# State space model's coefficients on four quarters of the array, and the last expert weights in fewer parts

## The chip, the cores and the metric

The kernel runs on one core of a Trainium2 chip. Its time is the device time of one execution in microseconds (us). Before the change it is 2480.15 us, the median of 3 runs (2478.76 to 2482.7). Engines are named as in the profile: PE is TensorE (PEld its weight loads), DVE VectorE, ACT ScalarE, POOL GpSimd, SP SyncE, which here issues most DMAs. Everything is computed in fp32; one fp32 matmul of the program is two MATMUL instructions in the trace, each with a weight load of its own.

## The reference

Two transformer-like blocks over 512 tokens of 1024 channels. The first has sparse attention beside a recurrent branch and an MLP. The second has a Fourier mix beside a state space model (SSM), and 64 experts, two per token. What matters here is one direction of the SSM, and the experts:

```
def _ssm_direction(ug, a_re, a_im, log_dt, b_re, b_im, c_re, c_im, reverse):
    lam = lax.complex(a_re, a_im);  dt = exp(log_dt)[:, None]
    a_bar = jnp.exp(lam * dt)                                  # 32 groups, 64 states
    b_bar = ((a_bar - 1.0) / lam)[..., None] * b_mat           # 16 channels per group
    bu = jnp.einsum('blgc,gnc->blgn', ug, b_bar)
    _, h = lax.associative_scan(_scan_combine, (a, bu), axis=1, reverse=reverse)
    return jnp.einsum('blgn,gcn->blgc', h, c_mat).real

def expert_block(args):
    xb, e = args
    a = jax.nn.silu(xb @ w_gate[e]) * (xb @ w_up[e])
    return a @ w_down[e]
```

It runs once forwards and once backwards, and the two are added. Everything that depends only on the weights (powers of a_bar, b_bar, C, and products of them) is a coefficient, independent of the tokens.

## The kernel before, in words

The program is written engine by engine; the order on each engine is the order of the code, and semaphores tie them together. PSUM has 8 banks of 512 columns; open_tile (L372) takes a bank and waits until its last user was evicted. Weights come in 2 MB loads into slots of SBUF, issued by SP in a fixed plan (L344 to L356); a load waits until the product that last used its slot has ended.

**Coefficients.** They are computed during the first block's MLP, woven (L135) into its first product, mlp_in, whose 32 dense tiles (8 matmuls of 128x512 each, L381) PE does one after the other. Both scans share the 128 partitions: the 64 states of the forward scan stand in rows 0 to 63, those of the backward scan in rows 64 to 127. BB holds b_bar (real and imaginary, 32 groups x 16 channels), CC holds C. The sequence is cut into blocks of 8 tokens, so for each group a 16 x 272 table z is needed: 128 columns from the one scan, 16 from both (the token itself), 128 from the other. In 8 steps c of four groups each:

- DVE and POOL form outer products of powers with BB and CC: Mr and Mi (to be transposed) and mb = MB2[c % 2], C times the powers; S("mcm") tells that mb is there (L1830 to L1842, L2258).
- PE transposes Mr and Mi, two banks (L660, L663), and after the next dense tile multiplies for z: for each group six matmuls into one bank of its own, in output rows 0 to 15 (L667 to L680). The operand on the array is BZ, a copy of BB with zeros in the other scan's rows, so that a product over all 128 rows takes one scan alone. Two groups come after one dense tile and two after the next.
- ACT evicts the transposes and each group's z (L1280) into Zt, and stores mbr, mbi, mcr, mci and z to DRAM, five stores per step, counted on st0 and st1 (16 each, so 80 per step; 320 in all on each).

BZ is zeroed by POOL (L2270) and filled by DVE with four copies (L1804, L1805). Zt is one buffer. SP, POOL and ACT wait for 320 on both counts before they go on to the second block.

**Experts.** 32 pairs of experts; a pair has six 2 MB matrices (gate, up, down for both), 192 loads through a ring of 9 slots (L2444 to L2458). pe_pair (L983) transposes the pair's rows, multiplies by gate and up (L1005), transposes, and multiplies by down (L1034). The two experts of a pair have 64 rows each and sit on the two halves of the array's columns. For the last pair the two up matrices are loaded in 8 parts of 512 KB, k by k and expert by expert (S("up0") to S("up3")), and the two down matrices in the same way ("last0" to "last3"); before either set SP waits for both slots (L2459 to L2470). PE takes them part by part (L1003, L1018; the down product at L1022). After it come DVE's and ACT's evictions (L2204, L1430), the spreading of the last pair's rows to the tokens by one-hot products (L981), DVE's sums with the rows that POOL gathers from y_d (L2128, L2320), and the final norm (L2212).

Of the kernel before, what the change touches and what calls it, by code (L numbers as in the profile page):

```python
# [16 lines left out]
PAIRS = 32  # L17
# [131 lines left out]
def program(nc, A, out):  # L149
    with ExitStack() as ctx:  # L150
# [36 lines left out]
        zone = al(53000 - at[0])  # L187
# [79 lines left out]
        BZ = view(zone, 20480, 4, 512)  # L267
        T1, T2, Mr, Mi = (view(zone, 20480 + 2048 + 512 * n, 512) for n in range(4))
        Zt = view(zone, 20480 + 4096, 1088)
# [108 lines left out]
        def tensor_program(pe):  # L378
# [272 lines left out]
            def ssm():  # L651
                yield from pause(8)
                flat = BB.rearrange("p a b c -> p a (b c)")
                for c in range(8):
# [12 lines left out]
                    for q in range(4):  # L667
                        gg = 4 * c + q
                        o = open_tile(pe, ("z", gg), any_bank())
                        cols = slice(16 * gg, 16 * gg + 16)  # L670
                        mm_ = (mb[:, 0, 128 * q:128 * q + 128], mb[:, 1, 128 * q:128 * q + 128])
                        for at0, n, zr, zi, rhs in (
                                (0, 128, BZ[:, 2, cols], BZ[:, 3, cols], mm_),
                                (128, 16, flat[:, 0, cols], flat[:, 1, cols], (CC[:, 0, gg, :], nC[:, cols])),
                                (144, 128, BZ[:, 0, cols], BZ[:, 1, cols], mm_)):
                            pe.matmul(o[0:16, at0:at0 + n], zr, rhs[0], start=True, stop=False)  # L676
                            ins = pe.matmul(o[0:16, at0:at0 + n], zi, rhs[1], start=False, stop=True)
                        ins.then_inc(T.f("z", gg), 1)
                        if q == 1:
                            yield  # L680
                    yield
# [301 lines left out]
        def pe_pair(pe, table, q, ready, weight, bank, gathered):  # L983
# [9 lines left out]
            for mat, name in enumerate(("g", "u")):  # L993
# [5 lines left out]
                for k in range(8):  # L999
                    if mat == 0 and k % 4 == 0:  # L1000
                        pe.wait_ge(*table.free("xt", q, k // 4))
                    if parts and k % 2 == 0:
                        pe.wait_ge(S(f"up{k // 2}"), 32)  # L1003
# [46 lines left out]
        def scalar_program(act):  # L1050
# [193 lines left out]
            def ssm():  # L1244
# [11 lines left out]
                for c in range(8):  # L1256
# [5 lines left out]
                    if c > 1:  # L1262
                        act.wait_ge(st, 80 * (c // 2))
# [1466 lines left out]
```

## Time and profile before

| | |
|---|---|
| three runs, median (lowest, highest) | 2480.15 us (2478.76, 2482.7) |
| the profiled execution | 2475.58 us, span 2473.8 us |
| mean granted TensorE clock | 0.967 |
| PE busy | 2260.6 us, 91% of the span |
| DVE, ACT, POOL busy | 613.6, 331.4, 208.9 us |
| moved by DMA | 552.44 MB |
| chain that ended last | PE 70%, DMA 24% |

The span runs from the first to the last instruction of the program. A busy share is an average over stages with different limits, so it says little about one stage. A row of the chain is a piece of work that the end of the kernel waited for; a row of the timeline gives start, duration, engine, line and operation, and in brackets how long the engine had been idle and what released it. In the windows PEclk is the granted clock as a share of 2.4 GHz, and the DMA share the mean over 16 engines.

### The profile page before, as it was taken

Reading aid. Unit: us, or ns where it says so; the run is one execution under the profiler, and the core shown is the slowest. Engines: PE = TensorE matmul, PEld = TensorE weight load, DVE = VectorE, ACT = ScalarE, POOL = GpSimd, SP = SyncE. Lnnn points to the kernel's source line nnn. Section 1 sums busy time; section 2 is a strip of 40 time slices with the busy share of each in tenths; the row PEclk is TensorE's granted clock in tenths of the full one; section 3 lists DMA queues with packets and bytes.
Section 4 is the critical chain, followed back from the end, with each engine's and each line's share of the span. In section 5 each row is a group of like instructions: output and inputs, shape, how many; then the busy total and the mean of one; then the engine's idle time right before and its main releaser. Section 6 shows DMA issues by size and latency. Waiting matters only on the chain.

```text
span 2473.8 us, 20406 instructions
## 1 busy us (share of the span) xinstructions
PE 2260.6 (91%) x8284; PEld 1048.6 (42%) x8284; DVE 613.6 (25%) x1315; ACT 331.4 (13%) x668; POOL 208.9 (8%) x187
## 2 busy tenths in 40 slices
PE   8999999999999999999999999988788888878786
PEld 5554444445455544457644454333333333333332
DVE  2146544301623130032631142111111111111114
ACT  2014424202111100021010030000000000000001
POOL 0001111010333200000000000000000000000001
PEclk9999999999999999998999999999999988898998
DMA  6201010322232221128432429999999999999995
GB/s 270 85 35 68 35 68 8 146 102 85 85 106 88 112 105 68 68 73 134 151 123 85 170 108 407 425 426 427 426 426 426 427 426 426 424 426 423 423 397 219
DMA packets 70288, 552.44 MB, mean 223 GB/s; under 512 B 21416, under 2 KB 25640, under 8 KB 38768
## 3 DMA queue, kind: packets, MB, share of 16 engines
q1 hardware_dynamic: 43680, 515.49, 51.3%
q10 hardware_dynamic: 16432, 23.23, 3.1%
q0 software_dynamic: 10080, 12.38, 1.4%
q8 instruction: 67, 1.10, 0.2%
q14 instruction: 29, 0.24, 0.0%
HBM read 543.91 MB, written 35.68 MB: 234 GB/s over the span
## 4 chain that ended last, share of the span: by engine, by line
PE 70%; DMA 24%; DVE 2%; SPq 1%; ACT 1%; issue 1%; DVEq 0%; POOL 0%; ACTq 0%; POOLq 0%
PE ps L381 25%; DMA sb<-in_eu 11%; PE ps L457 9%; PE ps L1005 8%; PE ps L697 8%; DMA sb<-in_eg 6%; DMA sb<-in_ed 6%; PE ps L1034 4%; PE ps L400 2%; PE ps L855 2%; PE ps L629 2%; PE ps L542 1%; PE ps L575 1%; PE ps L569 1%; PE ps L676 1%
## 5 line engine op out<-in xcount | busy, mean ns | idle before, releaser
L381 PE MATMUL ps<-sb 128*128 128x512 f32 (+2 forms) x1536 | 613.8, 559 | 2.9 <-issue 1.4
L1005 PE MATMUL ps<-sb 128*64 128x512 f32 x2048 | 478.6, 623 | 89.4 <-DMA sb<-in_eu 63.3
L381 PEld LDWEIGHTS ps<-sb 128*128 128x128 f32 x1536 | 279.7, 190 | 317.4 <-issue 314.2
L1005 PEld LDWEIGHTS ps<-sb 128*64 128x64 f32 x2048 | 175.0, 143 | 372.3 <-issue 372.2
L1034 PE MATMUL ps<-sb 128*64 128x512 f32 x992 | 249.5, 661 | 38.0 <-DMA sb<-in_ed 26.2
L457 PE MATMUL ps<-sb 128*128 128x512 f32 x512 | 238.2, 604 | 0.0
L697 PE MATMUL ps<-sb 128*128 128x512 f32 x448 | 192.5, 592 | 0.7 <-issue 0.7
L1034 PEld LDWEIGHTS ps<-sb 128*64 128x64 f32 x992 | 81.0, 151 | 185.0 <-issue 166.8
L1448 DVE TENSOR_TENSOR sb<-sb 128x32 f32<-128x32 f32 (+10 forms) x292 | 115.4, 412 | 136.6 <-PE ps L663 83.2
L457 PEld LDWEIGHTS ps<-sb 128*128 128x128 f32 x512 | 92.1, 191 | 101.0 <-issue 99.7
L697 PEld LDWEIGHTS ps<-sb 128*128 128x128 f32 x448 | 85.0, 190 | 107.7 <-issue 107.7
L2324 POOL DMA_INDIRECT y_d<-sb x31 | 31.2, 1007 | 854.0 <-PE ps L991 742.4
L1064 ACT ACTIVATE sb<-ps 128x512 f32<-128x512 f32 (+4 forms) x119 | 62.5, 532 | 268.1 <-PE ps L381 91.2
L2196 DVE SCALAR_TENSOR_TENSOR sb<-sb,ps 128x512 f32<-128x512 f32 x32 | 22.1, 690 | 273.4 <-PE ps L1005 273.4
L2191 DVE SCALAR_TENSOR_TENSOR sb<-sb,ps 128x512 f32<-128x512 f32 x32 | 22.1, 690 | 241.0 <-ACT sb L1420 241.0
L1472 DVE COPY sb<-ps 128x512 f32<-128x512 f32 (+6 forms) x53 | 34.5, 650 | 163.0 <-PE ps L381 89.8
L2241 POOL TENSOR_TENSOR sb<-sb 128x256 f32<-128x256 f32 (+3 forms) x32 | 41.6, 1301 | 381.8 <-DVE sb L1666 381.7
L2206 DVE COPY sb<-ps 128x512 f32<-128x512 f32 x31 | 21.5, 693 | 209.1 <-PE ps L1034 209.1
L2186 DVE TENSOR_TENSOR sb<-ps,sb 128x512 f32<-128x512 f32 x64 | 41.4, 687 | 101.9 <-PE ps L991 101.1
L1424 ACT ACTIVATE sb<-ps 128x512 f32<-128x512 f32 x32 | 19.2, 599 | 347.5 <-PE ps L1012 347.5
L400 PE MATMUL ps<-sb 128*128 128x256 f32 x256 | 58.6, 389 | 6.3 <-DVE sb L1467 3.5
L855 PE MATMUL ps<-sb 128*128 128x512 f32 x128 | 58.4, 598 | 1.6 <-DVE sb L1987 1.6
(286 smaller groups left out, 1554.3 us busy)
## 6 DMA issues: line engine op xcount, KB each, us to landing
sb<-in_eg SPq DMA_DIRECT2D x64, 2048.0 KB, 33.0
sb<-in_eu SPq DMA_DIRECT2D x62, 2048.0 KB, 33.7
sb<-in_ed SPq DMA_DIRECT2D x62, 2048.0 KB, 33.9
sb<-in_m SPq DMA_DIRECT2D x16, 2048.0 KB, 7.3
sb<-in_mg SPq DMA_DIRECT2D x8, 1536.0 KB, 6.9
sb<-in_winF SPq DMA_DIRECT2D x5, 2048.0 KB, 7.3
sb<-in_mgg SPq DMA_DIRECT2D x4, 2048.0 KB, 7.3
sb<-in_wo SPq DMA_DIRECT2D x4, 2048.0 KB, 7.3
```

The source lines that it names most:

```text
L381: ins = pe.matmul(out, lhsT, rhs, start=k == 0, stop=k == len(pieces) - 1)
L400: ins = pe.matmul(T.ap(*tile)[:, t], lhsT, rhs[:, t], start=k == 0, stop=k == 7)
L457: ins = pe.matmul(o, lhsT, rhs, start=k == 0, stop=k == 7)
L629: ins = pe.matmul(o, MG1[:, k, 128 * i:128 * i + 128], wo[nh][:, k, :], start=k == 0, stop=k == 7)
L697: ins = pe.matmul(acc[2 * i + nh], HT[:, k, 128 * i:128 * i + 128], w[:, q, 512 * nh:512 * nh + 512], start=k == 0, stop=False)
L855: ins = pe.matmul(T.ap(*name), MG2[:, k, 128 * i:128 * i + 128], wo[nh][:, k, :], start=k == 0, stop=k == 7)
L1005: ins = pe.matmul(o[64 * e:64 * e + 64, :], x[:, k, 64 * e:64 * e + 64], weight(2 * mat + e)[:, 512 * k:512 * k + 512], start=k == 0, stop ...
L1034: ins = pe.matmul(o[64 * e:64 * e + 64, :], aT[:, k, 64 * e:64 * e + 64], weight(4 + e)[:, d:d + 512], start=k == 0, stop=k == 3)
L1064: act.activation(dst, T.ap(*name) if src is None else src, ACT.Copy).then_inc(T.s(*name), 1)
L1448: return own(dve.tensor_tensor(o, a, b, op))
L2186: dve.tensor_tensor(XT[:, 4 * hf:4 * hf + 4, :], table.ap("xt", q, hf).rearrange("p (a b) -> p a b", a=4), bc(ck("gx")[:, 4 * hf:4 * hf + ...
L2241: pool.tensor_tensor(pr, pr, bc(ST[u % 4][:, 2:4], 2, nk), ALU.mult).then_inc(S("prob"), 1)
```

## The change

In the coefficients, the four groups of a step go to the four quarters of the array's columns, output rows 32q to 32q + 15, and each scan is multiplied with its own 64 rows alone, taken straight from BB; BZ, its memset and its copies go. Each step fills two banks, ("zb", c, 0) with the backward scan (128 columns) and the part of both scans (16 columns), and ("zb", c, 1) with the forward scan. ACT evicts each bank with one copy over all 128 partitions into Zt, which is now doubled, and issues four stores for z, one per group; the counts become 128 per step and 512 in all.

For the last pair, the first expert's up matrix comes in one load of 2 MB and the second's in two of 1 MB; the first's down matrix in one of 2 MB and the second's in parts of 1 MB, 512 KB and 512 KB. Each expert's load waits for its own slot only. PE's waits are changed to match.

```diff
-        BZ = view(zone, 20480, 4, 512)
-        Zt = view(zone, 20480 + 4096, 1088)
+        Zt = [view(zone, 20480 + 4096 + 272 * n, 272) for n in range(2)]
...
@@ PE, ssm()
                     pe.wait_ge(S("mcm"), c + 1)
-                    for q in range(4):
-                        gg = 4 * c + q
-                        o = open_tile(pe, ("z", gg), any_bank())
-                        cols = slice(16 * gg, 16 * gg + 16)
-                        mm_ = (mb[:, 0, 128 * q:128 * q + 128], mb[:, 1, 128 * q:128 * q + 128])
-                        for at0, n, zr, zi, rhs in (
-                                (0, 128, BZ[:, 2, cols], BZ[:, 3, cols], mm_),
-                                (128, 16, flat[:, 0, cols], flat[:, 1, cols], (CC[:, 0, gg, :], nC[:, cols])),
-                                (144, 128, BZ[:, 0, cols], BZ[:, 1, cols], mm_)):
-                            pe.matmul(o[0:16, at0:at0 + n], zr, rhs[0], start=True, stop=False)
-                            ins = pe.matmul(o[0:16, at0:at0 + n], zi, rhs[1], start=False, stop=True)
-                        ins.then_inc(T.f("z", gg), 1)
-                        if q == 1:
-                            yield
-                    yield
+                    cols = [slice(16 * (4 * c + q), 16 * (4 * c + q) + 16) for q in range(4)]
+                    for way, rows_ in enumerate((slice(64, 128), slice(0, 64))):
+                        o = open_tile(pe, ("zb", c, way), any_bank())
+                        for ri in range(2):
+                            for q in range(4):
+                                ins = pe.matmul(o[32 * q:32 * q + 16, 0:128], flat[rows_, ri, cols[q]],
+                                                mb[rows_, ri, 128 * q:128 * q + 128], start=ri == 0, stop=ri == 1)
+                        if way == 0:
+                            for ri in range(2):
+                                for q in range(4):
+                                    rhs = nC[:, cols[q]] if ri else CC[:, 0, 4 * c + q, :]
+                                    ins = pe.matmul(o[32 * q:32 * q + 16, 128:144], flat[:, ri, cols[q]], rhs,
+                                                    start=ri == 0, stop=ri == 1)
+                        ins.then_inc(T.f("zb", c, way), 1)
+                        yield
...
@@ PE, pe_pair, the last pair's up
-                    if parts and k % 2 == 0:
-                        pe.wait_ge(S(f"up{k // 2}"), 32)
+                    if parts and k == 0:
+                        pe.wait_ge(S("up0"), 16)
+                    if parts and k % 4 == 0:
+                        pe.wait_ge(S(f"up{1 + k // 4}"), 16)
...
@@ and its down, for k in range(4)
-                    pe.wait_ge(S(f"last{k}"), 32)
+                    if k != 1:
+                        pe.wait_ge(S(f"last{max(k, 1)}"), 16)
+                    if k == 0:
+                        pe.wait_ge(S("last0"), 16)
...
@@ ACT, ssm()
-                    if c:
-                        act.wait_ge(S(f"st{(c - 1) % 2}"), 80 * ((c - 1) // 2 + 1))
-                    for q in range(4):
-                        gg = 4 * c + q
-                        copy(("z", gg), Zt[0:16, 272 * q:272 * q + 272], T.ap("z", gg)[0:16, 0:272])
-                        if q == 1:
-                            yield
-                    for q in range(4):
-                        act.wait_ge(*T.free("z", 4 * c + q))
-                    act.dma_start(z_d[:, gs, :], Zt[0:16, :].rearrange("p (a b) -> p a b", a=4)).then_inc(st, 16)
+                    copy(("zb", c, 0), Zt[c % 2][:, 0:144], T.ap("zb", c, 0)[:, 0:144])
+                    yield
+                    copy(("zb", c, 1), Zt[c % 2][:, 144:272], T.ap("zb", c, 1)[:, 0:128])
+                    for way in range(2):
+                        act.wait_ge(*T.free("zb", c, way))
+                    for q in range(4):
+                        act.dma_start(z_d[:, 4 * c + q, :], Zt[c % 2][32 * q:32 * q + 16, :]).then_inc(st, 16)
...
@@ DVE (its four copies into BZ and the wait for the memset go as well, and POOL's memset)
-                    dve.wait_ge(*T.full("z", 4 * (c - 2) + 3))
-                    dve.wait_ge(S(f"st{c % 2}"), 80 * (c // 2))
+                    dve.wait_ge(*T.full("zb", c - 2, 1))
+                    dve.wait_ge(S(f"st{c % 2}"), 128 * (c // 2))
...
@@ SP, the last pair
-            for e in range(2):
-                sp.wait_ge(*T.full(*W.ended[W.before[("ex", 6 * PAIRS - 4 + e)]]))
-            for k in range(4):
-                for e in range(2):
-                    sp.dma_start(slot("ex", 6 * PAIRS - 4 + e)[:, 1024 * k:1024 * k + 1024],
-                                 EW[1][2 * PAIRS - 2 + e][:, 1024 * k:1024 * k + 1024]).then_inc(S(f"up{k}"), 16)
...
+            for mat, sem, parts in ((1, "up", (2048, 2048)), (2, "last", (2048, 1024, 1024))):
+                n = 6 * PAIRS - 6 + 2 * mat
+                sp.wait_ge(*T.full(*W.ended[W.before[("ex", n)]]))
+                sp.dma_start(slot("ex", n), EW[mat][2 * PAIRS - 2]).then_inc(S(f"{sem}0"), 16)
+                sp.wait_ge(*T.full(*W.ended[W.before[("ex", n + 1)]]))
+                at_ = 0
+                for k, size in enumerate(parts):
+                    sp.dma_start(slot("ex", n + 1)[:, at_:at_ + size], EW[mat][2 * PAIRS - 1][:, at_:at_ + size]).then_inc(S(f"{sem}{k + 1}"), 16)
+                    at_ += size
```

## Rows read from the trace of the kernel before

**Rows 1.** The page: PE's busy row, and what the DMA engines moved in 40 slices.

```profile
PE 2260.6 (91%) x8284; PEld 1048.6 (42%) x8284; DVE 613.6 (25%) x1315; ACT 331.4 (13%) x668; POOL 208.9 (8%) x187
...
GB/s 270 85 35 68 35 68 8 146 102 85 85 106 88 112 105 68 68 73 134 151 123 85 170 108 407 425 426 427 426 426 426 427 426 426 424 426 423 423 397 219
```

**Rows 2.** The page: the chain that ended last, shares by engine.

```profile
PE 70%; DMA 24%; DVE 2%; SPq 1%; ACT 1%; issue 1%; DVEq 0%; POOL 0%; ACTq 0%; POOLq 0%
```

**Rows 3.** Chain in order of time, 690 to 720 us: start, us, piece.

```profile
690.73 0.44 PE ps L660 x4
...
691.60 6.87 PE ps L381 x16
698.47 0.32 PE ps L676 x2
698.79 0.22 PE ps L677 x2
...
699.05 0.05 PE ps L677 x2
...
700.52 7.06 PE ps L381 x16
...
716.70 0.44 PE ps L660 x4
```

**Rows 4.** Line L676: duration in ns, minimum, median, maximum, and shapes.

```profile
L676 PEld LDWEIGHTS ps<-sb x192: 92/96/97, 672.4 to 864.9; 128*16 128x16 f32 x192
L676 PE MATMUL ps<-sb x192: 176/270/283, 672.4 to 865.0; 128*16 128x128 f32 x128, 128*16 128x16 f32 x64
```

**Rows 5.** Timeline of PE: products on the two halves of the array.

```profile
2389.55 7.09 PE L1005 MATMUL ps<-sb 128*64 128x512 f32 x32 [0.94 <-DMA sb<-in_eg]
```

**Rows 6.** Waits from 640 to 895 us: total us, times, longest.

```profile
ACT sb L1241 <- PE ps L381: 174.5, 27, 6.7
...
DVE sb L1448 <- PE ps L663: 83.2, 6, 14.4
```

**Rows 7.** Waits of PE from 866 to 1490 us, the longest.

```profile
PE ps L400 <- DVE sb L1467: 3.5, 1, 3.5
...
PE ps L743 <- DMA sb<-mbi_d: 1.1, 1, 1.1
```

**Rows 8.** DMA issues by size: count, KB each, median us to landing.

```profile
sb<-in_ed SPq DMA_DIRECT2D x62, 2048.0 KB, 33.9
...
sb<-in_ed SPq DMA_DIRECT2D x8, 512.0 KB, 12.9
```

**Rows 9.** Timeline of the SP queue, 2384 to 2460 us.

```profile
2396.72 16.61 SPq L2463 DMA_DIRECT2D sb<-in_eu  x8
2413.43 13.53 SPq L2469 DMA_DIRECT2D sb<-in_ed  x8
```

**Rows 10.** Windows: us, PE, PEld, DVE, ACT, POOL busy; PEclk, DMA share, GB/s.

```profile
2405.00:2415.00 10.00, 8.37 (x42) 3.22 (x40) 1.01 (x2) 0.60 (x1) 0.00 (x0) 1.00 0.73 261
...
2425.00:2435.00 10.00, 9.06 (x45) 3.57 (x42) 1.38 (x2) 0.60 (x1) 5.01 (x5) 1.00 0.99 368
...
2445.00:2450.00 5.00, 2.75 (x8) 0.53 (x6) 0.00 (x0) 0.00 (x0) 0.00 (x0) 0.50 0.25 102
```

**Rows 11.** Timeline, 2434 to 2462 us: last down product (L1022) and VectorE.

```profile
2436.01 1.94 PE L1022 MATMUL ps<-sb 128*64 128x512 f32 x8 [0.69 <-ACT sb L1424]
...
2438.67 1.94 PE L1022 MATMUL ps<-sb 128*64 128x512 f32 x8 [0.72 <-DMA sb<-in_ed]
...
2443.55 1.28 DVE L2128 SCALAR_TENSOR_TENSOR sb<-sb 128x1024 f32<-128x1024 f32 x1 [1.26 <-DMA sb<-y_d,sb]
...
2443.77 2.73 PE L1022 MATMUL ps<-sb 128*64 128x512 f32 x8 [3.16 <-DMA sb<-in_ed]
...
2448.74 3.34 PE L1022 MATMUL ps<-sb 128*64 128x512 f32 x8 [2.25 <-DMA sb<-in_ed]
...
2450.77 0.75 DVE L2204 TENSOR_SCALAR sb<-ps,sb 128x512 f32<-128x512 f32 x1 [5.93 <-PE ps L1022]
```

More of the change, by code:

```diff
@@ L1262, in ssm @@
                     if c > 1:
-                        act.wait_ge(st, 80 * (c // 2))
+                        act.wait_ge(st, 128 * (c // 2))
                     if c == 0:
@@ L1292, in row_load @@
                 act.dma_start(row, A[name].partition_broadcast(P)).then_inc(S("row"), 16)
-            act.wait_ge(S("st0"), 320)
-            act.wait_ge(S("st1"), 320)
+            act.wait_ge(S("st0"), 512)
+            act.wait_ge(S("st1"), 512)
             act.wait_ge(S("ep"), 1)
@@ L1800, in vector_program @@
             after(tt(BB[:, 1], v32(Mr), v32(Mi), ALU.add))
-            flat = BB.rearrange("p a b c -> p a (b c)")
-            dve.wait_ge(S("bz_zero"), 1)
-            for ri in range(2):
-                own(dve.tensor_copy(BZ[0:64, ri, :], flat[0:64, ri, :]))
-                after(own(dve.tensor_copy(BZ[64:128, 2 + ri, :], flat[64:128, ri, :])))
             dve.tensor_scalar(nC, CC[:, 1].rearrange("p a b -> p (a b)"), -1.0, None, ALU.mult).then_inc(S("ssm_k"), 1)
@@ L2269, in ssm @@
                 pool.wait_ge(*T.full("wo1", 3, 1))
-                pool.memset(BZ, 0.0).then_inc(S("bz_zero"), 1)
                 yield
@@ L2282, in gpsimd_program @@
             weave(mlp_in(), ssm())
-            pool.wait_ge(S("st0"), 320)
-            pool.wait_ge(S("st1"), 320)
+            pool.wait_ge(S("st0"), 512)
+            pool.wait_ge(S("st1"), 512)
             pool.memset(Ep[:, 0, :, 0], 1.0).then_inc(S("ep_one"), 1)
@@ L2401, in sync_program @@
             sp.wait_ge(S("mg1"), 8)
-            sp.wait_ge(S("st0"), 320)
-            sp.wait_ge(S("st1"), 320)
+            sp.wait_ge(S("st0"), 512)
+            sp.wait_ge(S("st1"), 512)
             for g in range(2):
@@ L2458, in sync_program @@
                     load(("ex", n), EW[k // 2][2 * q + k % 2])
-            for e in range(2):
-                sp.wait_ge(*T.full(*W.ended[W.before[("ex", 6 * PAIRS - 4 + e)]]))
-            for k in range(4):
-                for e in range(2):
-                    sp.dma_start(slot("ex", 6 * PAIRS - 4 + e)[:, 1024 * k:1024 * k + 1024],
-                                 EW[1][2 * PAIRS - 2 + e][:, 1024 * k:1024 * k + 1024]).then_inc(S(f"up{k}"), 16)
-            for e in range(2):
-                sp.wait_ge(*T.full(*W.ended[W.before[("ex", 6 * PAIRS - 2 + e)]]))
-            for k in range(4):
-                for e in range(2):
-                    sp.dma_start(slot("ex", 6 * PAIRS - 2 + e)[:, 1024 * k:1024 * k + 1024],
-                                 EW[2][2 * PAIRS - 2 + e][:, 1024 * k:1024 * k + 1024]).then_inc(S(f"last{k}"), 16)
+            for mat, sem, parts in ((1, "up", (2048, 2048)), (2, "last", (2048, 1024, 1024))):
[7 more added lines that the diff above has]
+                    at_ += size
             sp.wait_ge(*T.full("g", PAIRS - 1))
```

## The prediction

> **What bounds the kernel now.** I read the page first: PE is busy for 91% of the span, and from slice 25 of 40 on the DMA engines move some 425 GB/s [rows 1]. The chain that ended last is PE for 70% and DMA for 24% [rows 2]. So two regimes follow each other: PE sets the time up to the experts, and the stream of expert weights sets it from there to the last pair. The stream's first loads wait for ring slots that earlier products release, so an earlier PE moves the stream forward as a whole.
>
> For the first edit I took the chain in order of time inside the MLP's first product, where the coefficients are woven in. The reader is to see that it is PE without a gap: dense tiles of 16 instructions (an fp32 matmul is two) in 6.87 to 7.06 us, and between them a half of a step's four groups, from 698.47 to 700.52 us [rows 3]. ACT and DVE wait for PE there, 174.5 and 83.2 us in all, DVE up to 14.4 us at a time [rows 6]. For the second edit I took the timeline of the last pair: the last down product waits three times for its parts [rows 11].
>
> **Edit 1, the products on quarters.** One of the 8 steps takes 716.70 - 690.73 = 25.97 us. Off go the transposes (0.87, from 690.73 to 691.60) and three dense tiles at 6.87: 4.49 us are left for the coefficients [rows 3]. A step holds 32 instructions with 128 columns (128 of L676 [rows 4] and as many of L677 over 32 groups are 8 per group) and 16 with 16 columns. The former cost 0.22 / 2 = 0.11 us, the latter 0.05 / 2 = 0.025 [rows 3]: 3.52 + 0.40 = 3.92. The other 0.57 I put down to the four changes between the full array and its 32-column tiles, 0.14 each.
>
> The changed step has just as many instructions, 32 and 16, so nothing is saved unless they overlap. Each matmul still streams 128 columns; half the rows make none of them shorter. What changes is that four of them in a row write four quarters of the array's columns, where now all sit in the first quarter. The nearest thing that the trace shows is the experts' product on halves: 32 instructions of 512 columns take 7.09 us [rows 5], where 16 full ones take 6.87 [rows 3]. Two halves thus run side by side at next to no loss. It shows no quarters, and none on 64 rows with 32 columns. Bounds: none overlap, 3.52 us; all four do, 0.88. In between, two at a time, 1.76. I take 0.88, since the halves come within 4% of their ideal, and since four instructions per 0.11 us is 0.027 each, not quicker than the 0.025 at which the small ones already follow each other. For the small ones I keep 0.40 (bound below 0.10 for full overlap; above, 0.40). The changes of tile become five (64 rows, 128 rows, full, 64 rows, full): 0.71. The sum is 0.88 + 0.40 + 0.71 = 1.99 us against 4.49, so 2.50 saved per step and **20.0 us** over eight. With the small ones overlapped too it would be 22.4; two at a time, (4.49 - 1.76 - 0.40 - 0.71) x 8 = 13.0; no overlap, 4.49 - 4.63 = -0.14 per step, a loss of 1.1 us.
>
> The weight loads stay one per instruction. One of them takes 95 ns and lies beside the instruction before it [rows 4]. The Trainium skill (TensorE: Matmul & The Clock Gate, Part 3, What overlaps and what doesn't) speaks against this change: it says that a weight load overlaps running matmuls only where the row group differs, and the four quarters share their rows. The trace disagrees for halves, which share all 128 rows and still pack [rows 5]; for quarters it shows nothing. The same page (Measured speedup vs the span model) gives 2.38 for three column tiles; an estimate with that efficiency is 3.52 / 3.17 = 1.11 us per step in place of 0.88, and 1.8 us less gain.
>
> What the rest of edit 1 touches lies off the path. ACT makes two copies per step in place of four and issues four stores in place of one, 24 issues more in all, in a stage in which it waits for PE for 174.5 us [rows 6]; behind them in its queue stand the Relu evictions of the dense tiles, which have all other banks of the ring to be late in. A step needs 4 banks in place of 6. The waits on the stores count to 512 in place of 320; what they gate (POOL's and DVE's table of powers, SP's next loads) has the MLP's whole second product before it is needed. DVE loses four copies and the wait for POOL's memset, where it already is ahead of PE [rows 6]. All at nothing; if DVE were late, its own slack of up to 14.4 us per step would have to go first, and the steps shrink by 2.5.
>
> Does the gain survive? From 866 to 1490 us PE's longest wait is 3.5 us, for DVE; the one for a DMA is 1.1 us, behind a load that a product itself releases [rows 7]. All of this moves with PE. I carry the 20.0 whole.
>
> **Edit 2, the last weights.** Now 16 transfers of 512 KB, issued in 16.61 and 13.53 us [rows 9]; 2.1 and 1.7 us each, while SP is held. Changed: one of 2 MB and two of 1 MB for up; one of 2 MB, one of 1 MB and two of 512 KB for down. Seven issues, and the first waits for its own slot only. In the windows in which small parts are moved, the engines' share falls to 0.73 with 261 GB/s, and at share 0.99 they move 368 GB/s, where the slices before show 424 or so [rows 1, 10]. A 2 MB load takes 33.9 us to land, at 4.9 us each (2.10 MB at 426 GB/s) [rows 1, 8]: seven are under way, so low shares mean that some engines have run dry while others are behind, and a load lands with the slowest. Feeding the fast ones better therefore doesn't help by itself; bigger pieces do. 8.4 MB at 368 GB/s are 22.8 us; half of it at 426, 3.1 MB halfway at 397 and 1.05 MB at 368 are 20.6: **2.2 us**. The last parts moreover land 5.1 and 5.0 us apart (2438.67, 2443.77, 2448.74 [rows 11]), twice what 1.05 MB needs, since the gathers of the rows of y share the engines; parts that land earlier leave less beside them.
>
> The end sees it through two waits. The last product's four parts start at 2436.01, 2438.67, 2443.77 and 2448.74 and run 1.94, 1.94, 2.73 and 3.34 us, the last with a granted clock of 0.50, the lower level of 1.2 GHz, from 2445 to 2450 [rows 10]. Without any wait the product would take 7.1 us (as 32 instructions on halves do, [rows 5]), end at 2443.1 and gain 9.0 us: the upper bound. But DVE takes the gathered rows first, until 2443.55 + 1.28 = 2444.83, and only then evicts the product, now at 2450.77 [rows 11]; with the gathers where they are, 5.9 is the most. The lower bound is 0: were the transfers no faster at all, part 1 would wait for six of the eight half megabytes and start about when the third does now, 2443.77; four parts at 1.77 us end at 2450.9, not after 2452.1. So the coarser first part costs nothing by itself. I take **4.5 us**, between 2.2 and 5.9, nearer to the latter since a late part also costs the lower clock (3.34 us in place of 1.77). SP's other queue entry, the final norm's row, follows seven issues and not sixteen; it is needed last.
>
> **Sum.** 20.0 + 4.5 = 24.5 us. The profiled execution took 2475.6 us, its span 2473.8: it would take 2451.1. The three timed runs have a median of 2480.15, 4.6 higher, which I leave in: 2480.15 - 24.5 = **2455.7 us**.
>
> **Rivals.** (a) Only two quarters run at a time, because each fp32 matmul is two instructions on one tile and matmuls start in order. For it: they are issued tile by tile. Against: on halves the order is the same and nothing is lost. 13.0 + 4.5: 2462.7. (b) Nothing overlaps, because the array takes one such tile at a time. Only the end gains: 2480.15 + 1.1 - 4.5 = 2476.8. (c) The end gains nothing, as the gathers then hold what the weights did: 2460.2. (d) The other side: the weight loads of quarters that share rows are not hidden, as the page above has it. Each of 32 instructions then costs 0.095 + 0.11; 3.04 us more per step than with no overlap, 24.3 in all: 2480.15 + 1.1 + 24.3 - 4.5 = 2501. It decides from 0.08 us of unhidden load per instruction on, in a step that doesn't overlap.
>
> **Chances.** The forecast 0.67; (a) 0.11, (b) 0.06, (c) 0.12, (d) 0.04. The range reaches from both upper bounds, 2480.15 - 22.4 - 5.9 = 2451.9, less 2 should the gathers come earlier as well, to (a) with half of the end's gain, 2464.9: 2450 to 2465. A measurement of this kernel can tell about 0.2%, 5.0 us. Forecast, (a) and (c) are faster: 0.90; (b) is 3.4 us off, no change: 0.06; (d) 0.04.
>
> **What would show it.** Right: in the chain, a step of some 23.5 us where it was 25.97, PE busy on the quarters' lines with starts far closer than 0.11 us, the MLP's second product starting 20 us earlier; at the end three or four waits of the last product with small ones left, and DVE's eviction some 4 us earlier, counted from the last pair's start. Wrong: starts 0.11 us apart (b), pairs (a), loads ahead of each instruction (d), or a first wait of the down product that grows by what the later ones lose. If the MLP's second product starts 20 us earlier and the experts' stream does not, the step that failed is the one that carries the gain on.

## The result, and the profile after

Four timed runs of the changed kernel gave 2443.15 to 2451.36 us, median 2447.72, beside four of the kernel before with a median of 2479.45: ratio 0.987, interval 0.9842 to 0.9897. It is faster, by 31.7 us between the medians, where 24.5 were forecast; the time lies 8.0 us under the forecast and 2.3 us under the range. Five more rounds (below) give 25.8 us by their ratio and 24.3 us by their medians. So two things need an explanation: the size of each edit's gain, and what was wrong with the base from which they were taken off.

The page after: PE's busy row, the data rates and the chain's shares, against [rows 1, 2].

```profile
PE 2226.5 (91%) x8284; PEld 1022.6 (42%) x8284; DVE 612.2 (25%) x1311; ACT 323.1 (13%) x652; POOL 206.8 (8%) x186
...
GB/s 273 86 35 69 35 69 4 151 103 78 95 118 79 141 77 72 101 52 161 155 102 83 159 156 408 426 426 426 425 426 426 426 427 427 425 425 422 421 426 221
...
PE 69%; DMA 26%; DVE 3%; ACT 1%; issue 1%; DVEq 0%; POOL 0%; SPq 0%; ACTq 0%; POOLq 0%
```

PE has just as many instructions and is busy 34 us less. SP's issuing, 1% of the chain before, is at 0%.

The chain after in order of time, 680 to 720 us (start, us, piece), against [rows 3].

```profile
683.48 0.44 PE ps L659 x4
683.92 0.44 PE ps L662 x4
684.36 6.87 PE ps L380 x16
691.23 0.56 PE ps L673 x16
691.78 0.21 PE ps L679 x16
692.00 7.06 PE ps L380 x16
699.06 0.56 PE ps L673 x16
699.62 7.06 PE ps L380 x16
706.68 0.44 PE ps L659 x4
```

A step is 706.68 - 683.48 = 23.20 us, where it was 25.97: 2.77 less, for which 2.50 was forecast. The 16 instructions of a way (one of the two scans) take 0.56 us, the 16 small ones (16 columns, both scans) 0.21. The trace also has their starts: the 16 of a way come in four sets of four, 7 ns apart within a set and 0.11 us from one set to the next (0, 7, 14, 20, then 120, 127, 133, 140 ns). So the four quarters stream at the same time.

For the whole span I cut the run at four places of the code and take the first start of each line from the trace (duration in ns, minimum, median, maximum; first and last start; the lines answer to those of before in the second fence). They are the first transposes of the coefficients, the MLP's second product, the experts' products and the last down product. After:

```profile
L659 PE MATMUL ps<-sb x32: 272/272/273, 660.1 to 822.8; 128*128 128x128 f32 x32
L698 PE MATMUL ps<-sb x448: 592/592/667, 839.5 to 1031.4; 128*128 128x512 f32 x150
L1008 PE MATMUL ps<-sb x2048: 592/592/1117, 1469.3 to 2410.1; 128*64 128x512 f32 x187
L1028 PE MATMUL ps<-sb x32: 592/592/1117, 2415.6 to 2423.6; 128*64 128x512 f32 x32
```

Before:

```profile
L660 PE MATMUL ps<-sb x32: 272/272/273, 664.6 to 846.7; 128*128 128x128 f32 x32
L697 PE MATMUL ps<-sb x448: 592/592/667, 866.2 to 1058.1; 128*128 128x512 f32 x150
L1005 PE MATMUL ps<-sb x2048: 592/592/1117, 1493.1 to 2433.1; 128*64 128x512 f32 x187
L1022 PE MATMUL ps<-sb x32: 592/643/1115, 2436.0 to 2451.4; 128*64 128x512 f32 x32
```

| stretch | before | after | less |
|---|---|---|---|
| up to the first transposes | 664.6 | 660.1 | 4.5 |
| to the MLP's second product (edit 1) | 201.6 | 179.4 | 22.2 |
| to the experts' first product | 626.9 | 629.8 | -2.9 |
| to the last down instruction (edit 2) | 958.3 | 954.3 | 4.0 |
| to the end of the span | 22.4 | 21.8 | 0.6 |

The sum is the 28.4 us between the spans. Edits 1 and 2 hold 26.2 of it. The first and the third row have no changed instruction of PE in them. The copies and the memset that are gone from the first had ended 8 us before the transposes, and PE waited for neither.

The end after: the SP queue (start, us), against [rows 9].

```profile
2366.09 0.43 SPq L2461 DMA_DIRECT2D sb<-in_eu  x1
2374.33 0.80 SPq L2465 DMA_DIRECT2D sb<-in_eu  x2
2375.18 0.43 SPq L2461 DMA_DIRECT2D sb<-in_ed  x1
2383.17 1.94 SPq L2465 DMA_DIRECT2D sb<-in_ed  x3
```

SP was held for 16.61 and 13.53 us by sixteen issues; seven take 3.6 us in all. And the last pair's products with VectorE, against [rows 11].

```profile
2403.64 7.09 PE L1008 MATMUL ps<-sb 128*64 128x512 f32 x32 [0.78 <-DMA sb<-in_eu]
...
2415.59 8.57 PE L1028 MATMUL ps<-sb 128*64 128x512 f32 x32 [3.19 <-DMA sb<-in_ed]
...
2421.63 1.29 DVE L2126 SCALAR_TENSOR_TENSOR sb<-sb 128x1024 f32<-128x1024 f32 x1 [1.22 <-DMA sb<-y_d,sb]
2423.34 0.75 DVE L2202 TENSOR_SCALAR sb<-ps,sb 128x512 f32<-128x512 f32 x1 [0.43 <-PE ps L1028]
```

The last down product waits once, 3.19 us, and then runs through; before it was four pieces with three waits. VectorE's last gathered row of y ends at 2422.92, and 0.43 us later the product's first half is evicted, so the gathers now are nearly the limit. They have moved as well: counted from the experts' first product the last gathered row ends at 953.6 us (2422.92 - 1469.3), where it ended at 951.7 before.

The windows beside the last loads (us, PE, PEld, DVE, ACT, POOL busy; PEclk, DMA share, GB/s), against [rows 10].

```profile
2390.00:2400.00 10.00, 8.33 (x44) 3.55 (x42) 1.67 (x3) 0.60 (x1) 0.99 (x1) 1.00 0.64 263
2400.00:2410.00 10.00, 9.22 (x44) 3.51 (x42) 0.69 (x1) 0.60 (x1) 4.98 (x5) 1.00 0.70 261
2410.00:2420.00 10.00, 5.86 (x22) 2.15 (x20) 4.14 (x4) 0.60 (x1) 3.00 (x4) 0.83 0.81 321
```

The windows show no higher rate with larger parts: 261 to 321 GB/s here, where small ones had 261 to 368. When the last part lands says more, and it does move (below, with the last weights).

### The profile page after: what moved, and what is told of

Read it like the earlier page. It is cut to its first block, busy times and chain, and to the rows that moved or that the text cites. A ratio compares the mean times of both kernels' runs of the same rounds, so it can differ in the third digit from the quotient of the medians.

```text
span 2445.4 us, 20383 instructions
## 1 busy us (share of the span) xinstructions
PE 2226.5 (91%) x8284; PEld 1022.6 (42%) x8284; DVE 612.2 (25%) x1311; ACT 323.1 (13%) x652; POOL 206.8 (8%) x186
## 4 chain that ended last, share of the span: by engine, by line
PE 69%; DMA 26%; DVE 3%; ACT 1%; issue 1%; DVEq 0%; POOL 0%; SPq 0%; ACTq 0%; POOLq 0%
PE ps L380 25%; DMA sb<-in_eu 12%; PE ps L1008 9%; PE ps L456 8%; DMA sb<-in_eg 8%; PE ps L698 8%; PE ps L1040 4%; DMA sb<-in_ed 4%; PE ps L399 2%; PE ps L856 2%; PE ps L628 2%; PE ps L541 1%; PE ps L574 1%; PE ps L568 1%; DMA sb<-in_mgg 1%
## 5 line engine op out<-in xcount | busy, mean ns | idle before, releaser
L1008 PE MATMUL ps<-sb 128*64 128x512 f32 x2048 | 487.7, 632 | 108.6 <-DMA sb<-in_eu 79.3
L1008 PEld LDWEIGHTS ps<-sb 128*64 128x64 f32 x2048 | 176.7, 145 | 398.8 <-issue 398.7
L1040 PE MATMUL ps<-sb 128*64 128x512 f32 x992 | 232.5, 623 | 26.9 <-ACT sb L1427 17.2
L1451 DVE TENSOR_TENSOR sb<-sb 128x32 f32<-128x32 f32 (+10 forms) x292 | 115.4, 412 | 115.7 <-PE ps L662 66.2
L1040 PEld LDWEIGHTS ps<-sb 128*64 128x64 f32 x992 | 73.7, 143 | 164.2 <-issue 137.6
L1070 ACT ACTIVATE sb<-ps 128x512 f32<-128x512 f32 (+4 forms) x103 | 54.6, 538 | 252.6 <-PE ps L380 90.9
```

Of the source, the lines that this page charges most:

```text
L1008: ins = pe.matmul(o[64 * e:64 * e + 64, :], x[:, k, 64 * e:64 * e + 64], weight(2 * mat + e)[:, 512 * k:512 * k + 512], start=k == 0, stop ...
L1040: ins = pe.matmul(o[64 * e:64 * e + 64, :], aT[:, k, 64 * e:64 * e + 64], weight(4 + e)[:, d:d + 512], start=k == 0, stop=k == 3)
L1070: act.activation(dst, T.ap(*name) if src is None else src, ACT.Copy).then_inc(T.s(*name), 1)
L1451: return own(dve.tensor_tensor(o, a, b, op))
```

## The experiments

Three theories after the first result. **A**: each edit gives what its own stretch shows, and the rest of the difference is where stretches of the lower clock fall. **B**: the start and the MLP give what was forecast and the end gives some 11. **C**: something beyond the two edits' places became faster.

**The two edits apart, and both kernels again.** The first has this of the diff and not the new parts of the last weights:

```diff
-                        o = open_tile(pe, ("z", gg), any_bank())
...
-                            pe.matmul(o[0:16, at0:at0 + n], zr, rhs[0], start=True, stop=False)
...
+                    for way, rows_ in enumerate((slice(64, 128), slice(0, 64))):
+                        o = open_tile(pe, ("zb", c, way), any_bank())
...
+                                ins = pe.matmul(o[32 * q:32 * q + 16, 0:128], flat[rows_, ri, cols[q]],
+                                                mb[rows_, ri, 128 * q:128 * q + 128], start=ri == 0, stop=ri == 1)
```

> The kernel before with the products on quarters alone; the last weights go in their old 16 parts. Theory A (each edit gives what its own place in the trace shows, and the rest of the difference between the medians is where stretches of the lower clock fall): a step takes 23.2 us in place of 25.97, 22.2 to 22.6 us over eight, ratio 0.991. Theory B (the start and the MLP give what was forecast, 20.0, and the end gives the rest, some 11): ratio 0.992, and the other half alone 0.995 to 0.996. Theory C (something beyond the two edits' own places became faster, by 5 us or so): this kernel or the one with the new tail alone shows more than its place gives: 27 us or more here, ratio 0.989 or less.

The second has the other half:

```diff
-            for k in range(4):
-                for e in range(2):
-                    sp.dma_start(slot("ex", 6 * PAIRS - 4 + e)[:, 1024 * k:1024 * k + 1024],
...
+            for mat, sem, parts in ((1, "up", (2048, 2048)), (2, "last", (2048, 1024, 1024))):
```

> The kernel before with the last weights in fewer parts alone. Theory A: 4 to 4.5 us, ratio 0.998, the last down product in one go and its eviction 4 us earlier counted from the last pair's start. Theory B: 10 us or more, ratio 0.996 or less. Rival (c) of the prediction: nothing, ratio 1.000.

The third and fourth are the two kernels unchanged.

> The changed kernel once more, five rounds beside the kernel before. Theory A: the two edits add, 22.4 + 4.3 = 26.7 us, ratio 0.989 (the 31.7 us between the medians of the first comparison were 5 too many). Theory B and C: 31 us, ratio 0.987.

> The kernel before against itself: ratio 1.000 by every theory; its interval says what five rounds can tell. If stretches of the lower clock fall differently from run to run, as theory A has it, single runs spread over 5 us or more while the steps in the trace stay at 25.97 us.

| kernel | median us | ratio to before | interval |
|---|---|---|---|
| before, 23 runs | 2474.89 | | |
| quarters alone | 2454.93 | 0.991 | 0.9892 to 0.9928 |
| last weights alone | 2471.95 | 0.9986 | 0.9969 to 1.0003 |
| after again | 2450.62 | 0.9896 | 0.9881 to 0.9911 |
| before again | 2476.64 | 1.0001 | 0.9984 to 1.0019 |

0.9 and 0.14% make 1.04%, and both together measure 1.04%: this fits two edits that add, though with intervals of 0.15 to 0.18% to either side the exact agreement is luck. On 2475 us that is 22.3 + 3.5 = 25.8 us. The ratios are not quotients of the medians, which lie 20.0, 2.9 and 24.3 us under that of before. B and C wanted 31 for both; the interval of the third, 22.0 to 29.5 us, excludes it. The last weights alone can't be told from nothing by their times; their own stretch of the trace can (below). Of the 31.7 us in the first comparison some 6 to 7 were the luck of four runs on each side: the kernel before gave 2469.93 to 2488.41 us in its other runs here, one stray record of 7777.8 us aside.

The stretches say what that luck is. The quarters alone, profiled at 2463.97 us:

```profile
L659 PE MATMUL ps<-sb x32: 272/273/273, 674.2 to 836.9; 128*128 128x128 f32 x32
L698 PE MATMUL ps<-sb x448: 592/592/668, 853.5 to 1045.4; 128*128 128x512 f32 x150
```

Edit 1's stretch is 853.5 - 674.2 = 179.3 us, as in the kernel after. But its first transposes start at 674.2 and not at 660.1, in code that is the same. Some 6 of these 14 us are lost between 100 and 160 us. This window of this kernel (columns as before):

```profile
100.00:160.00 60.00, 58.61 (x253) 39.20 (x251) 17.44 (x50) 5.78 (x18) 0.00 (x0) 0.89 0.31 123
```

and of the kernel after:

```profile
100.00:160.00 60.00, 57.15 (x274) 35.67 (x273) 22.61 (x69) 7.72 (x20) 0.00 (x0) 1.00 0.31 123
```

A granted clock of 0.89 is the lower level, 1.2 GHz, in part of the window: 0.11 x 60 = 6.6 us of work at full clock are missing, and PE got through 21 fewer instructions. Over the fourteen profiled executions shown here the first transposes start at 659.5 to 674.2 us with no changed instruction of PE ahead of them, while edit 1's stretch takes 201.6 to 201.7 (before, before again, last weights alone) or 179.3 to 179.4 (after, after again, quarters alone).

The clock's records account for most of it. The work at full clock that is missing in the first stretch (its length times one less its granted clock) is 0 us in after and in last weights alone, 3.4 in nine kernels, before among them (start 664.6 to 665.0), 6.8 in two quarters (666.2), 8.5 in halves (671.1) and 11.9 in quarters alone (674.2). Less this, all fourteen start at 659.4 to 662.6. In edit 1's stretch nothing is missing in any of them. That the lower stretches fall at other places in each execution is shown; what makes them fall there is open.

**How many quarters work at once.** All four groups on one quarter, then on two, with the same instructions on 64 rows:

```diff
+                        for hi in range(4 // NQ):
+                            for ri, q in [(a, NQ * hi + b) for a in range(2) for b in range(NQ)]:
+                                p_, f_ = 32 * (q % NQ), 128 * (q // NQ)
+                                ins = pe.matmul(o[p_:p_ + 16, f_:f_ + 128], flat[rows_, ri, cols[q]],
+                                                mb[rows_, ri, 128 * q:128 * q + 128], start=ri == 0, stop=ri == 1)
```

Here NQ is 1 or 2; groups on the same quarter write their own column ranges of the bank.

> The changed kernel, but all products on one quarter of the array's columns: the four groups of a way write four column ranges of one bank in its partitions 0 to 15, group after group, still on 64 rows; the small products have a bank of their own. If the overlap of the four quarters is what shortens the step: 16 instructions of 0.109 us take 1.75 us per way in place of 0.56, the small ones about 0.40 in place of 0.21, a step 25.8 us (23.20 + 2.4 + 0.2), which is the old 25.97 again. If it were the half rows: 23.2 as in the changed kernel.

> As the one before, on two quarters, two groups side by side and then the other two. If tiles side by side cost nothing until the array is full: 0.88 us per way and a step of 23.9 us. If a part of the quarters' gain came from elsewhere (a pair that is issued 5 ns apart but streams one after the other): more than 0.95 per way.

The chain, one quarter (L674 a way, L683 the small ones):

```profile
717.93 6.87 PE ps L380 x16
724.79 1.85 PE ps L674 x16
726.64 0.49 PE ps L683 x16
```

and two quarters:

```profile
715.47 6.87 PE ps L380 x16
722.34 0.98 PE ps L674 x16
723.32 0.30 PE ps L683 x16
```

1.85, 0.98 and (with four, above) 0.56 us per way: 16 instructions at 0.109 are 1.75, 0.875 and 0.4375, and 0.10, 0.10 and 0.12 are left. Edit 1's stretch takes 202.5 us on one quarter, 186.9 on two, 179.4 on four, 201.6 before. So the half rows are worth nothing by themselves, and the whole gain is the overlap of the quarters' columns. In both kernels the small products have a bank of their own, which the lines above don't show. The two runs came out at 2473.70 and 2460.75 us, one time each.

**The order of the products.** The loops over group and over real and imaginary part change places, for both kinds of product:

```diff
-                        for ri in range(2):
-                            for q in range(4):
+                        for q in range(4):
+                            for ri in range(2):
```

> The changed kernel with the order turned round: real and imaginary part of one group one after the other, then the next group; the same instructions on the same quarters. If each quarter works off instructions of its own while the others wait (my theory, from the two passes of one fp32 matmul, which come in a row on one quarter and yet lose nothing): a step of 23.2 to 23.6 us. If matmuls start strictly in order, the second matmul of a group holds up the next group, and pairs remain: 1.3 us or more per way in place of 0.56, a step of 24.7 or more.

```profile
712.53 6.87 PE ps L380 x16
719.39 0.58 PE ps L673 x16
719.97 0.23 PE ps L679 x14
```

0.58 in place of 0.56, with four instructions in a row on the same quarter. If each had to start behind its forerunner in the program, a quarter's first instruction would wait for the third of the quarter before it to end: 4 x 3 x 0.109 + 0.109 = 1.42 us per way. It takes 0.58 with the change of tiling in it. The starts say the same: four within 40 ns (0, 14, 27 and 40), the next at 120, where one quarter alone gives a start each 109 ns. So a quarter works off its own instructions while the next quarter's start. Rival (a) rested on that strict order, and it is refuted. The one run took 2452.16 us. (The chain names 14 of the 16 small instructions; some records are missing there and in the padded kernel below.)

**Half rows or columns.** The four quarters again, but with the zero-padded operands on 128 rows that the kernel before had:

```diff
-                                ins = pe.matmul(o[32 * q:32 * q + 16, 0:128], flat[rows_, ri, cols[q]],
-                                                mb[rows_, ri, 128 * q:128 * q + 128], start=ri == 0, stop=ri == 1)
+                                ins = pe.matmul(o[32 * q:32 * q + 16, 0:128], BZ[:, 2 - 2 * way + ri, cols[q]],
+                                                mb[:, ri, 128 * q:128 * q + 128], start=ri == 0, stop=ri == 1)
```

> The changed kernel with its products on four quarters, but on 128 rows as in the kernel before, half of them zeros. If only the quarters of the columns count: 0.56 us per way, a step of 23.2 us or a little less (one change of the row tiling fewer ahead of the small ones). If the 64 rows are needed for the overlap: 1.85 us per way and a step of 25.8.

```profile
719.02 0.56 PE ps L674 x16
719.57 0.10 PE ps L680 x15
719.67 7.06 PE ps L381 x16
```

The ways still take 0.56, so the rows are not needed for the overlap. And the small products take 0.10 in place of 0.21: they now follow without a change of the row tiling. This gives the two parts of a block: streaming, shared over the tiles, and 0.1 us each time that the tiling changes. TensorEngine Tiling (Array Packing) of the Trainium skill, Tiling Modes, says that changing the tiling mode drains the engine while tiles of one mode run independently; the trace agrees, at 0.11 us for this change. Going back to the full array costs more: the first dense tile after a block takes 7.06 where others take 6.87, 0.19 us, in every kernel here. Edit 1's stretch: 843.4 - 664.9 = 178.5, 0.9 less than with half rows. The one run took 2450.01 us.

**Both ways side by side.** Half rows do allow what padding doesn't: the two ways use different rows, so with two banks all eight tiles can run at once. The small products follow, and no dense tile stands between the ways any more.

```diff
+                    ob = [open_tile(pe, ("zb", c, way), any_bank()) for way in range(2)]
+                    for ri in range(2):
+                        for way, rows_ in enumerate((slice(64, 128), slice(0, 64))):
+                            for q in range(4):
+                                ins = pe.matmul(ob[way][32 * q:32 * q + 16, 0:128], flat[rows_, ri, cols[q]],
+                                                mb[rows_, ri, 128 * q:128 * q + 128], start=ri == 0, stop=ri == 1)
...
```

> The changed kernel with both ways of a step in a row and the small products behind them, with no dense tile between the two ways; the two ways use different rows and different banks. One return to the full array falls away per step. If ways on different rows overlap as quarters do, the two take together 0.56 us or little more in place of 1.12: some 0.7 us less per step, 5 to 6 us over all, ratio to the kernel before 0.987. If only the change of tile is saved: 0.19 us (the first dense tile after a block takes 7.06 where others take 6.87), 1.5 us over all, ratio 0.989. If DVE or ACT become late: waits for them at the transposes and nothing gained.

```profile
710.88 6.87 PE ps L380 x16
717.75 0.58 PE ps L673 x32
718.33 0.21 PE ps L679 x16
```

32 instructions in 0.58 us, where 16 take 0.56. Edit 1's stretch is 839.0 - 664.9 = 174.1 us, 5.3 less than after. Median 2444.67 us, ratio to before 0.9862, interval 0.9835 to 0.9888, where the changed kernel had 0.9896. The two intervals overlap a little, and they were measured on different chips, so the times alone don't part the two kernels; the stretch does, which takes 174.0 to 174.1 us in all four kernels with merged ways. DVE still waits for PE there, 61.8 us. By its stretch this version beats the changed kernel by 5.3 us, and it beats the kernel before by both.

**The last weights.** Three kernels, all with merged ways: the last four loads whole; all four in halves; and the sizes of the change with the old wait for both slots before the first issue. PE's waits are changed to match.

```diff
-            for mat, sem, parts in ((1, "up", (2048, 2048)), (2, "last", (2048, 1024, 1024))):
+            for mat, sem, parts in ((1, "up", (4096,)), (2, "last", (4096,))):
```

> The kernel with merged ways, and all four last loads whole, 2 MB each: no parts at all. From the experts' first product to the issue of the last down matmul the old tail takes 958.0 to 958.8 us and the new one 954.2 to 955.9. If the new tail gains because the last bytes land together, on all engines at once, and parts only let SP be free sooner: 954 to 956, the same again. If the parts that are left still start the last products early: 1 MB more to wait for, 2 to 3 us more, 957 to 958.

```diff
+                for h in range(2):
+                    for e in range(2):
+                        sp.dma_start(slot("ex", n + e)[:, 2048 * h:2048 * h + 2048],
+                                     EW[mat][2 * PAIRS - 2 + e][:, 2048 * h:2048 * h + 2048]).then_inc(S(f"{sem}{h}"), 16)
```

> The kernel with merged ways, and each of the last four loads in two halves of 1 MB, first half of both experts, then second half of both; up and down alike, eight issues. If a load lands with its slowest engine whatever its size: 954 to 956 us again, the second half landing with the first. If a first half can land 2.5 us (1 MB at 426 GB/s) before the second: the down product starts 2 to 3 us earlier, waits in its middle, and the end comes 1 to 2 us earlier, 952 to 954.

```diff
+                for e in range(2):
+                    sp.wait_ge(*T.full(*W.ended[W.before[("ex", n + e)]]))
-                sp.wait_ge(*T.full(*W.ended[W.before[("ex", n + 1)]]))
```

> The kernel with merged ways and the new sizes of the last loads, but the first of each pair waits for both slots, as in the kernel before. If the sizes alone make the end's gain: 954 to 956 us. If the earlier first issue makes it: 957.5 or more. I expect some 956 to 957, for the first up load is issued 9 us later.

From the first expert product to the last down instruction, worked out for each trace from rows as in the second fence pair; and, from the same start, when the last part of the down weights has landed (its last completion in the trace):

| last loads | last instruction, us | last part lands, us |
|---|---|---|
| before; before again; quarters alone | 958.3; 958.8; 958.0 | 955.6; 956.1; 956.6 |
| after; after again; last weights alone | 954.3; 955.9; 954.3 | 951.1; 951.8; 951.1 |
| one quarter; two; group by group; merged; padded (same loads) | 954.2; 954.4; 955.4; 954.4; 954.6 | 950.9; 951.3; 951.0; 951.1; 951.5 |
| whole | 957.3 | 947.8 |
| halves | 955.9 | 951.1 |
| both slots first | 955.7 | 951.6 |

The change's loads make this stretch 958.4 - 954.7 = 3.7 us shorter, means over three and eight traces; the two sets don't overlap. Their last part lands 956.1 - 951.2 = 4.9 us earlier. With the whole loads, four transfers, the last one lands earlier still, and yet they give most of the gain back (one trace, as for each of the last three rows). The kernel with whole loads, last up product and last down product:

```profile
2405.39 9.93 PE L1009 MATMUL ps<-sb 128*64 128x512 f32 x32 [3.34 <-DMA sb<-in_eu]
...
2417.67 8.78 PE L1028 MATMUL ps<-sb 128*64 128x512 f32 x32 [0.69 <-ACT sb L1427]
```

Now the up product waits 3.34 us for its load, where it waited 0.78, and starts at 936.8 us, where merged has 934.4; the down product doesn't wait at all for its own. The parts of the up load are what starts the last pair early; the theory that parts only free SP falls. The kernel with halves has these rows in SP's queue, in which the wait for the second slot, 8.3 us in either, stands between the first issue and the second:

```profile
2363.50 9.99 SPq L2461 DMA_DIRECT2D sb<-in_eu  x4
2373.53 15.44 SPq L2461 DMA_DIRECT2D sb<-in_ed  x4
```

The issues themselves take 1.6 and 7.0 us of it. The down product starts 2.5 us earlier (943.8 us after the first expert product, where merged has 946.3) but stops in its middle, for its second half:

```profile
2411.85 3.65 PE L1025 MATMUL ps<-sb 128*64 128x512 f32 x16 [0.99 <-DMA sb<-in_ed]
2419.26 5.35 PE L1025 MATMUL ps<-sb 128*64 128x512 f32 x16 [3.75 <-DMA sb<-in_ed]
```

That half lands at 951.1 us, as late as the last quarter of merged, and more of the product is left then. So its end isn't earlier, against my hope for 952 to 954. The waiting for both slots first shows 955.7, inside what the change's own loads scatter (954.2 to 955.9), and its last part lands at 951.6, though its first up load is issued at 904.0 us after the first expert product and that of after at 896.8. So the sizes are enough for nearly all of the earlier landing; whether the earlier first issue adds the last few tenths, one trace can't tell. The three came out at 2446.16, 2448.62 and 2445.24 us (the last from one run); none beats the merged kernel's 2444.67, which was timed on another chip.

## Why the prediction was right or wrong

**The base, wrong by 4.6 us.** This is the step that failed: the larger of two mis-sized terms in the 8.0 us. The prediction works from the profiled execution, 2475.6 us, and adds the 4.6 us to the median of three runs, "which I leave in". The 23 runs of before on one chip have a median of 2474.89: the profiled execution was the typical one and the three runs were late. From 2475.6 the sum gives 2451.1, which it states; after again measures 2450.62, and that median would lie inside the range. The first four runs of the changed kernel were 2.9 us lower, which no edit made.

**Edit 1, right in mechanism, 2.2 us too small.** Forecast 20.0, measured 22.2 in its stretch. The four quarters overlap fully, 0.88 us of streaming in two ways, as taken. The changes of tile at 0.71 hold in sum: 1.71 us are left of the 23.20 beside transposes and three dense tiles at 6.87, and 1.71 - 0.88 - 0.10 = 0.73. They aren't 0.14 each, though: 0.11 or 0.12 into a tiling of part of the array, three times, and 0.19 back to the full one, twice. The term that was mis-sized is "for the small ones I keep 0.40": they overlap as well, down to 0.10 us by themselves. The reason I gave, that four instructions per 0.11 us are not quicker than the pace of the small ones, mistook the streaming time of one quarter for a limit on issuing. The bound that I worked out for this case, 22.4, is what came.

**The weight loads.** Hidden, as the trace of the halves suggested [rows 5]. Rival (d) falls: in the merged kernel 32 instructions with 32 weight loads of 93 ns (median) are done in 0.58 us. The rule of that page (TensorE: Matmul & The Clock Gate of the Trainium skill, Part 3, What overlaps and what doesn't), by which a load overlaps running matmuls only where the row group differs, is contradicted by the padded run, where all share 128 rows: 16 instructions with 16 loads of 96 ns (median) in 0.56 us. Even if four quarters loaded side by side, loads that ran beside no matmul would make four times 0.096 + 0.109, 0.82 us. The 2.38 of the same page (Measured speedup vs the span model) for three column tiles, 0.79 each, is near the 1.85 / 0.56 = 3.3 for four, 0.83 each; but that ratio holds the change of tiling, which the sum had as a term of its own, and the 1.8 us that it would have taken off did not go.

**What was costed at nothing.** ACT's 24 more issues and DVE's missing copies cost and gave nothing: PE's only wait between 640 and 845 us is one of 0.7 us at the second product's start, and the trace of before has 0.7 there too, and DVE's for PE went from 83.2 to 66.2 us [rows 6].

**Whether the gain survives, right.** The stretch up to the experts is 626.6 to 626.9 us in the two traces of before and 623.0 to 629.8 in the others. Less the work at full clock that its lower stretches cost (5.1 to 13.7 us), it is 616.4 to 616.7 in the three traces without edit 1 and 615.7 to 617.9 in the eleven with it; the experts' stretch does not grow.

**Edit 2, right in size, half right in its picture.** Forecast 4.5, measured 3.7 to 4.0 in its stretch; up to the end of the span it is 5.1, or 4.0 without before again, whose tail held a stretch of the lower clock. The limit by the gathers was the right one to look for: they end 0.43 us ahead of the eviction. But I put it at 5.9 "with the gathers where they are", and they end 1.9 us later than before, which leaves 4.0. That bigger pieces help is borne out, though not by the windows' rates: the last part lands 4.9 us earlier, by the sizes nearly alone, where the sum gave the transfers 2.2. At the product three waits (0.72, 3.16 and 2.25 us) become a single one of 3.19 at its start, where I expected several small ones.

**The range.** Its low end was made of the terms alone, 2451.9 less 2, with no room for the scatter of the base and of four runs. With the base and the small products mended the forecast would have been 2455.7 - 4.6 - 2.2 = 2448.9, 1.2 us from the result and 1.7 from after again, less than four runs can tell.

## What to carry to other kernels

Small fp32 products that share a bank should write different quarters of the partitions, and where operands allow it use different halves of the rows in another bank: the streaming time divided here by the number of tiles (up to eight), and what remained was 0.1 us for each change of the tiling and 0.19 for the return to the full array, so gather them in one block. Compare a sum with stretches of the trace that end at unchanged instructions; a difference of medians over four runs carried here 6 us that no edit had made. And when a profile and a few timed runs differ by less than their scatter, a forecast should keep both bases in its range.

## What the hardware showed that I had not expected

- Eight tiles (two row halves by four column quarters) run as one: 32 instructions in 0.58 us, against 0.56 for 16 on four.
- Sixteen instructions of 16 columns on four quarters take 0.10 us, 6 ns each; issuing doesn't limit them at the 25 ns at which they follow each other on one quarter.
- The order of instructions among quarters hardly matters: 0.58 against 0.56 us.
- A 2 MB load is done by most DMA engines long before the last. For the first of the last up loads of the kernel after, the sixteen completions in the trace come 0, 0.1, 0.2, 0.3, 0.5, 1.4, 1.5, 1.8, 5.2, 7.7, 10.9, 13.5, 20.2, 21.2, 22.7 and 23.2 us after the first. DMA: Bandwidth & Descriptors of the Trainium skill (iDMA fabric — 4 AXI ports for 8 engines, asymmetric across TPBs) says in passing, in an explanation that it calls unconfirmed, of two cores that share memory ports, that a bulk load runs at the pace of its slowest engine; the trace agrees for one core: a product can't start before the last four engines are done.
- An issue isn't always short for SP. Of the eight up parts of before the first four were issued in 0.33 to 0.43 us each, the fifth in 1.8 and the last three in 4.2 to 4.4. In the kernel with halves six of the eight issues of 1 MB took 0.33 to 0.43 us, the fifth 2.3 and the last 3.9. The seven issues of 512 KB to 2 MB in the kernel after took 0.33 to 1.1. That points to how many transfers are under way rather than their bytes. This was seen, not tested.
